# Attention inside a hybrid trunk step: heads taken in order 0, 2, 1, 3, scores issued as pairs of two key heads, values as stationary operand, and the result left transposed for the output projection

## The reference

```python
HEAD_DIM = 64; ATTN_HEADS = 4; KV_HEADS = 2; ATTN_BLOCK = 128; WINDOW = 128
...
def one_block(b):
    parts = [einsum('bqkgd,bckd->bkgqc', qblk, k_ctx)]                # 128 context keys
    if local:                                                        # latent queries only
        s_loc = einsum('bqkgd,bskd->bkgqs', qblk, k_blk)             # up to 3 x 128 keys
        parts.append(where(valid, s_loc, -inf))
    p = softmax(concatenate(parts + [sink_logit], axis=-1), axis=-1)
    out = einsum('bkgqc,bckd->bqkgd', p[..., :c_len], v_ctx)
    if local:
        out = out + einsum('bkgqs,bskd->bqkgd', p[..., c_len:...], v_blk)
    return out
```

## Time and profile before

| | |
|---|---|
| median of 3 runs | 1483.44 us (1482.91 to 1487.77) |
| span of the profiled execution, first to last instruction | 1481.4 us |
| PE busy | 1254.5 us, 85% of the span |
| DVE, ACT, POOL busy | 709.7, 282.3, 114.1 us |
| chain that ended last | PE 53%, DMA 24%, DVE 11% |
| granted TensorE clock, mean | 0.927 |

### The profile page before, as it was taken

How to read it: one execution, slowest core, us unless ns; L and a number is a source line. 1 busy time by engine, 2 the same in 40 slices (tenths; PEclk the granted TensorE clock), 3 DMA queues, 4 the chain that set the end, 5 groups by cost and what they waited for, 6 DMA issues and landing times.

```text
span 1481.4 us, 20556 instructions
## 1 busy us (share of the span) xinstructions
PE 1254.5 (85%) x7762; PEld 864.0 (58%) x7762; DVE 709.7 (48%) x1579; ACT 282.3 (19%) x708; POOL 114.1 (8%) x171
## 2 busy tenths in 40 slices
PE   5999999888986797998849999988799579889792
PEld 2765577657862565565437556766578356465550
DVE  2256866782356132332363686677443633223324
ACT  0211132651111000000022104256211100000000
POOL 2000000001000211111000000000100011111100
PEclk9999999999987898999979999999999679899996
DMA  9221101247049999999761110014822389999985
GB/s 383 117 89 44 70 1 57 112 185 295 29 168 361 386 415 420 420 418 418 311 242 47 71 57 29 1 67 170 344 84 97 132 349 413 420 419 416 412 333 233
DMA packets 58179, 334.61 MB, mean 226 GB/s; under 512 B 11392, under 2 KB 11392, under 8 KB 23900
## 3 DMA queue, kind: packets, MB, share of 16 engines
q1 hardware_dynamic: 42336, 294.94, 49.4%
q0 software_dynamic: 15744, 38.34, 6.7%
HBM read 322.41 MB, written 27.61 MB: 236 GB/s over the span
## 4 chain that ended last, share of the span: by engine, by line
PE 53%; DMA 24%; DVE 11%; issue 4%; ACT 3%; DVEq 2%; SPq 1%; PEld 1%; ACTq 0%; POOL 0%; PEldq 0%; POOLq 0%
DMA U<-in_stream 14%; PE bank L1664 12%; PE bank L2033 10%; PE bank L1600 8%; PE bank L1923 7%; PE bank L2067 5%; DMA ring<-in_stream 5%; DMA RAB<-mod_rows 2%; PE bank L1765 1%; PE bank L1939 1%; DVE U L1203 1%; PE bank L1705 1%; DMA U<-moe_out 1%; PE bank L2015 1%; SPq L350 1%
## 5 line engine op out<-in xcount | busy, mean ns | idle before, releaser
L2033 PE MATMUL bank<-U,HT 128*64 128x256 f32 (+2 forms) x1248 | 211.6, 415 | 27.5 <-DMA U<-in_stream 22.8
L2033 PEld LDWEIGHTS bank<-U,HT 128*64 128x64 f32 (+2 forms) x1248 | 142.0, 154 | 82.7 <-issue 54.4
L1664 PE MATMUL bank<-HT,ring 128*128 128x512 f32 (+1 forms) x640 | 175.4, 435 | 2.1 <-issue 2.1
L1923 PE MATMUL bank<-ring,HT 128*128 128x256 f32 x640 | 150.6, 397 | 14.6 <-DVE U L1254 9.0
L1600 PE MATMUL bank<-ring,HT 128*128 128x256 f32 x640 | 151.7, 390 | 6.0 <-ACT HT L603 4.2
L1923 PEld LDWEIGHTS bank<-ring,HT 128*128 128x128 f32 x640 | 127.0, 201 | 34.8 <-issue 11.2
L1664 PEld LDWEIGHTS bank<-HT,ring 128*128 128x128 f32 x640 | 97.3, 191 | 79.8 <-issue 79.8
L1600 PEld LDWEIGHTS bank<-ring,HT 128*128 128x128 f32 x640 | 121.2, 195 | 23.0 <-ACT HT L603 4.1
L2033 PE MATMUL bank<-ring,HT 128*64 128x256 f32 (+2 forms) x608 | 119.8, 418 | 14.3 <-DMA ring<-in_stream 11.7
L1043 DVE SCALAR_TENSOR_TENSOR U<-U,prm 128x655 f32<-128x655 f32 x120 | 107.8, 898 | 5.9
L2067 PE MATMUL bank<-ring,HT 128*64 128x512 f32 (+2 forms) x224 | 100.3, 625 | 5.1 <-DMA U<-in_stream 5.1
(11 more groups left out here) (347 smaller groups left out, 1614.0 us busy)
## 6 DMA issues: line engine op xcount, KB each, us to landing
ring<-in_stream SPq DMA_DIRECT2D x140, 1024.0 KB, 10.3
U<-in_stream SPq DMA_DIRECT2D x108, 1024.0 KB, 17.1
RAB<-in_stream SPq DMA_DIRECT2D x18, 1024.0 KB
U<-moe_out SPq DMA_DIRECT2D x20, 512.0 KB, 7.3
RAB<-mod_rows POOLq DMA_DIRECT2D x12, 512.0 KB, 11.9
moe_in<-CAT POOLq DMA_DIRECT2D x10, 512.0 KB, 2.9
X<-in_x SPq DMA_DIRECT2D x1, 2560.0 KB, 15.3
out_y<-X SPq DMA_DIRECT2D x5, 512.0 KB, 6.8
```

The source lines that it names most:

```text
L1664: ins = e.matmul(out, wt(q)[:, k, P * (n % 2):P * (n % 2) + P], HT[:, k, lo:lo + w], start=(k == 0), stop=(k == KD - 1))
L1923: ins = e.matmul(PS[4 + n % 2][:, 256 * j:256 * j + 256], HT[:, k, t * P:(t + 1) * P], wt(q + j)[:, k, :], start=(k == 0), stop=(k == KD - 1))
L2033: ins = e.matmul(PS[2 + p][s, FF * j:FF * j + FF], xgT[:, p, k, s], wt(key)[:, k, :], start=(k == 0), stop=(k == KD - 1))
```

## The change

`HEADS = (0, 2, 1, 3)` is the order in which heads are taken. `scores(t, g)` issues the products of query heads g and 2 + g together, which use key heads 0 and 1 and so partitions 0 to 63 and 64 to 127, into two banks. `values(t)` is one call for a block: the value columns of a key head are the stationary operand (64 columns) and the transposed probabilities of its two query heads move (256 columns), so that the result stands transposed in bank 5, one key head on each half of the partitions. Since a per-query factor then runs along the free axis, `factors(t)` spreads the inverted sums over 64 partitions by four products with the identity, ACT copies them to `facs`, and DVE multiplies by them. The first two pieces of the concatenated result are already transposed, so the output projection reads them from CAT; the rows of its weight are permuted to fit on the host. Waits on one bank or another move with this (`att_fs` in place of `pj_sb` for the gate's banks), and some semaphores are joined.

```diff
-        PTs = view(TMP + 2048, 2, 4, P)
+        PTs = (view(TMP + 2048, 4, 2, P), view(2560 + 4 * 512, 4, 2, P))
+        facs = view(TMP + 3072, 2 * P)
...
+        def factor_bank(t):
+            return PS[6 + t % 2] if t + 1 < NT else PS[3]
...
                 for t in range(NT):
-                    for h in range(QH):
-                        if t:
-                            e.wait_ge(S["att_pt"], 20 * l + 4 * (t - 1) + h + 1)
-                        A(Pm[:, h, 0:w], PS[h][:, 0:w], ACT.Exp, ...)
-                    A(es[:, t, :], es[:, t, :], ACT.Exp).then_inc(S["att_es"], 1)
+                    for h in HEADS[:3]:
+                        exps(t, h)
+                    probs_out(t, HEADS[0])
+                    exps(t, HEADS[3])
+                    A(es[:, t, :], es[:, t, :], ACT.Exp).then_inc(S["att_exp"], 1)
                     e.wait_ge(S["pj_ps"], 10 * l + NT + t + 1)
                     A(CAT[:, t, 256:768], PS[6 + t % 2][:], ACT.Copy).then_inc(S["pj_sb"], 1)
-                    probs_out(t, 0)
                     if t == NT - 1:
-                        for n in range(3):
+                        for n in range(2):
                             columns_out(n)
-                    probs_out(t, 2)
+                    probs_out(t, HEADS[2])
+                    if t == NT - 1:
+                        columns_out(2)
+                    e.wait_ge(S["att_f"], NT * l + t + 1)
+                    A(facs, factor_bank(t)[:, 0:256], ACT.Copy).then_inc(S["att_fs"], 1)
...
+                    tap(2)
+                    probs_out(t, HEADS[1])
+                    e.wait_ge(S["att_exp"], 25 * l + 5 * t + 5)
+                    e.tensor_tensor(den, sums[:, t, :], es[:, t, :], ALU.add); dr()
+                    e.reciprocal(rden, den).then_inc(S["att_den"], 1)
...
+                    e.wait_ge(S["att_pv"], NT * l + t + 1)
+                    e.wait_ge(S["att_fs"], NT * l + t + 1)
+                    e.tensor_tensor(CAT[:, t, 0:256], PS[5][:, 0:256], facs, ALU.mult).then_inc(S["att_o"], 1)
...
+                def factors(t):
+                    if t:
+                        e.wait_ge(S["att_o"], NT * l + t)
+                    e.wait_ge(S["att_den"], NT * l + t + 1)
+                    e.wait_ge(S["pj_sb"], 10 * l + NT + t + 1)
+                    for g in range(2):
+                        for kv in range(KVH):
+                            ins = e.matmul(factor_bank(t)[64 * kv:64 * kv + 64, g * P:(g + 1) * P],
+                                           rden[:, 2 * kv + g:2 * kv + g + 1].to_broadcast((P, HD)), ident[:], ...)
...
+                def values(t):
+                    nb = [0] if t == 0 else [-1] + near(t)
...
                     for i, j in enumerate(nb):
-                        ins = e.matmul(PS[5][:, 64 * h:64 * h + 64], PTs[:, h % 2, i, :], v, ...)
+                        for kv in range(KVH):
+                            k = slice(64 * kv, 64 * kv + 64)
+                            ins = e.matmul(PS[5][k, 0:256], v, PTs[kv][:, i].rearrange("p a b -> p (a b)"), ...)
...
-                    turned_tile(t, "ct_ps", ("ct_sb_a", "ct_sb_d"), (0, 1, 6, 7, 2, 3, 4, 5))
+                    turned_tile(t, "ct_ps", ("ct_sb_a", "ct_sb_d"), (6, 7, None, None, 2, 3, 4, 5))
...
+                            rows = CAT[:, t, k * P:(k + 1) * P] if k < 2 else HT[:, k, t * P:(t + 1) * P]
```

More of the change, by code:

```diff
@@ L38 @@
 ROUNDS = list("PPFPFQBPBPPFBQBBPP")
+HEADS = (0, 2, 1, 3)
 SLOT = 2048
@@ L1091, in tap @@
                     done[0] = min(62, done[0] + n)
-                for h in range(QH):
+                for h in HEADS:
                     att_max(0, h)
@@ L1693, in _, with scores @@
                 e.wait_ge(S["ch_sb"], 8 * (l + 1))
[L1695 to L1698 removed]
+                def scores(t, g):
+                    rows = [(kv, slice(64 * kv, 64 * kv + 64), PS[2 * kv + g]) for kv in range(KVH)]
                     if t == 0:
[L1700 removed]
+                        for kv, r, bank in rows:
+                            ins = e.matmul(bank[:, 0:P], qkT[r, g, 0:P], qkT[r, 2, 0:P], start=True, stop=True)
                     else:
@@ L1766, in head @@
                     ins.then_inc(S["att_pv"], 1)
-                for h in range(QH):
-                    scores(0, h)
+                rden = small(108, QH)
+                for g in range(2):
+                    scores(0, g)
                 for i in range(4):
@@ L1772, in _ @@
                 for t in range(NT):
-                    for h in range(QH):
-                        head(t, h)
+                    if t + 1 < NT:
+                        fill = [lambda i=i: gate_part(4 * t + 4 + i) for i in range(4)]
+                    else:
+                        fill = [lambda i=i: columns(i) for i in range(4)]
+                    turned_probs(t, HEADS[0])
+                    fill[0]()
+                    turned_probs(t, HEADS[1])
+                    if t + 1 < NT:
+                        scores(t + 1, 0)
+                    else:
+                        fill[1]()
+                    turned_probs(t, HEADS[2])
+                    if t + 1 < NT:
+                        fill[1]()
+                    else:
+                        fill[2]()
+                    turned_probs(t, HEADS[3])
+                    if t + 1 < NT:
+                        scores(t + 1, 1)
+                    factors(t)
+                    fill[2 if t + 1 < NT else 3]()
+                    values(t)
+                    if t + 1 < NT:
+                        fill[3]()
+                columns(4)
                 columns(5)
```

140 lines of the change are left out of this document (63 added, 77 removed).

## The result

The changed kernel takes 1464.34 us (median of 4 runs, 1459.94 to 1466.35) against 1483.18 us for the kernel before (4 runs, 1482.83 to 1487.77) on the same chip. The quotient of these two medians is 0.9873. The ratio on record is 0.9842, with a 95% interval of 0.9817 to 0.9867; the record doesn't say how its runs are weighted. So the saving is 18.8 us by the medians and 23.4 us by the ratio. The forecast was 1461.1 in a range of 1453 to 1471, a ratio of 0.985.

What follows compares the result with a forecast made beforehand. TensorE's instructions were taken to bound attention blocks 0 to 3. Savings of 9.0 + 1.7 (last block) + 0.45 (projection) = 11.15 us a layer, 22.3 in all, gave 1461.1 us, range 1453 to 1471.

Steps and rivals of the forecast that it cites:

- case (a): Whole run: half-array products overlap and the whole saving reaches the end; 1461.1 us, range 1453 to 1467, chance 0.73.
- Blocks 0 to 3: Attention's first four query blocks, bound by TensorE: savings of 1.19, 2.45, 2.90 and 2.46 us, together 9.0 a layer.
- 0.15 for the turn, so 0.51: Context part of a score pair: 0.36 us for four alternating records plus 0.15 for turning to half rows, against 0.82.
- The rule on packs: Context pair by the skill's rule, one matmul plus some 4 ns a tile: 0.22 us, whole sum near 1456.5.
- Rival (c): Attention scores: pairs do not overlap, columns do; 2.5 + 4.3 us a layer lost, 1474.7 us, chance 0.07.
- Factors: Each attention block: four added products of 64 by 128, eight records, cost 0.50 us; alone they would be 0.88.
- Last block, to L1830: Last attention block, decided by hand-offs: 9.6 us against 10.46 before, with TensorE waiting 1.9 for ScalarE's gate copy.
- TensorE's own 2.2 us end last, and 0.7 goes: Barrier before the mixer: VectorE, last by 0.72 us, finishes earlier, so TensorE ends last and 0.7 us is saved.
- Projection: Output projection: two of eight transposes go per block; only the last two blocks' count, 4 x 0.11 = 0.45 us.
- Rival (b): Attention blocks 1 to 3: VectorE's copy or the exponential becomes the wait, beyond 1.5 us margin; 1470 us, chance 0.12.
- Rival (d): Attention: neither row nor column halves overlap; 3.85 us a layer more, 1491 us, chance 0.04.
- Rival (e): Last attention block: granted clock falls to 1.2 GHz; some 3 us a layer lost, 1468 us, chance 0.04.

Runs made afterwards that it cites:

- e2: Changed kernel with each score pair issued one key head after the other (context, latent, masks), same products and banks; 1482.79 us, ratio 0.9979.
- e9: Changed kernel with the output projection transposing eight pieces per block again, two of them unread; 1464.31 us, ratio 0.9843.
- e7: Changed kernel with score products and value products both issued one key head after the other; 1487.29 us, ratio 1.0.
- a2: The changed kernel run again, nothing edited, beside the kernel before on its own chip; 1461.35 us, ratio 0.9841.
- a3: The changed kernel run once more, unedited, in another set beside the kernel before; 1462.54 us, ratio 0.9842.
- e1: Changed kernel with ScalarE's gate copy moved ahead of its first probability copy in every block; 1457.02 us, ratio 0.9815.
- g2: Repeat, in another set, of the changed kernel with ScalarE's gate copy ahead of its first probability copy; 1462.78 us, ratio 0.9829.
- g3: Changed kernel with the gate copy first and the second of ScalarE's three last copies done by VectorE; 1459.59 us, ratio 0.9809.
- e3: Changed kernel with the value products of key head 0 over all key blocks first, then those of key head 1; 1470.22 us, ratio 0.9884.
- e4: Changed kernel with each block's four factor products issued twice; 1472.43 us, ratio 0.9889.

## Why the prediction was right, step by step

The time and the likeliest case (a) were right: TensorE's price in blocks 0 to 3, brought down by overlap, and passed on to the end. The sum came out nearly right too, in part by luck, since its terms were off in both directions.

- **Blocks 0 to 3, 9.0 a layer forecast, 9.85 measured** (1.53 + 2.73 + 3.10 + 2.49). Shown, since undoing the overlap gives the gain back. The step "0.15 for the turn, so 0.51" for the context pair was mis-sized: it made the narrow pair dearer than one head (0.41 in the same view), and the pair costs no more than one head. Context and latent pair together take 1.07 us where 0.51 + 0.65 = 1.16 was forecast. By their starts the eight pairs save 7.6 us where 6.8 was forecast. The value groups save 0.4 more than forecast and the factors cost 0.36 more; transposes, gate and masks come out even. The rule on packs that was weighed there (the Trainium skill, "TensorE: Matmul & The Clock Gate", Part 3) has a pack cost about what one of its tiles costs, which e2 bears out for this pair (0.33 for one head and 0.32 to 0.33 for two), but not its total of 1456.5, since it had 0.22 as the price of one. Latent pairs (one head's price) and values (1.88 forecast, 1.88 measured) were right. Rival (c), pairs that don't overlap, was not the case; e2, which takes their overlap away, prices it at 8.45 us a layer where 6.8 was forecast.
- **Factors, 0.50 forecast, 0.58 measured**, and 0.44 for a repeated set: the shape's pace was right, the start on top of it was missed.
- **Last block, to L1830: 9.6 forecast, 9.76 measured** at full clock, with the wait of 1.9 forecast at 1.77. The step that fell is "TensorE's own 2.2 us end last, and 0.7 goes": 3.22 became 2.94 or 2.95, so 0.27. ScalarE's copies of the product end last at the barrier and moving one of them away gains only 0.05. Together 0.97 a layer, not 1.7.
- **Projection, 0.45 forecast, 0.43 measured** (e9). The other six transposes were worth nothing, as said: the gate vector ends that stage. That the stage would last 1.2 and 1.6 us less in the profile after was in no term, and why it did is open.
- **Rival (b)**, VectorE, was not the case: one more tap per block costs 0.28 us a layer, two cost 2.4. The margin of 1.5 us was right for block 2 (1.4), and too wide for blocks 1 (0.7) and 3 (1.2).
- **Rival (d)**, no overlap at all and slower, 1491 forecast. With both orders undone the kernel ties with the one before (ratio 1.0). e7 is not quite that rival: the rival had no overlap of columns at all, while column halves that stand one behind the other still overlap partly, and the factors were left in turns (0.58 a block, not 0.88).
- **Rival (e)**, the lower clock in the last block, was put at 3 us a layer with a chance of 0.04. It happened in layer 0 of three of four profiled executions with this attention, and cost 0.83 us (the profile after), 1.16 (a2) and 1.14 (e9); layer 1 and both layers of a3 were free of it. So it was far likelier than forecast and far cheaper, and that it did no harm to the sum is luck. The condition for being wrong, "if the last block grows past 10.5 us", was met in all three (10.59, 10.92, 10.90), but by the clock and not by the hand-offs. That the wait of 1.77 us brings the fall on is argued, not shown: of the 20 last blocks with it 11 had a fall, of the six without it (e1, g2, g3) none.
- **The sum of 22.3 against the runs.** At full clock the attention and the projection give 2 x (9.85 + 0.97 + 0.43) = 22.5 us, the sum forecast within 0.2. What the runs gained is less certain than that: 18.8, 25.6 and 29.1 us between the medians of the three sets, where the kernel before alone ranges from 1477.25 to 1495.74, and 23.4 by the ratio. The spans of the profile after and of before differ by 16.8. There 20.8 came from the attention, 2.8 from the wait stages and 0.4 net from the start and the end; the mixers at a lower clock took 5.1 back and the rest of layer 0 2.1. Only the attention and the projection's 0.9 were in the sum. a3, whose attention was free of a lower clock, gives 22.0, but there too 2.7 from the wait stages happened to cover the 2.4 of the mixers. That the median of the first set is short of the sum by such falls of the clock is argued from profiled executions, not shown.
- **The stream of tiles moved**, as it had to: the longest wait of layer 0's experts, 29.46 us from 702.15, is 29.63 us from 694.33 after. By then the execution was 7.8 us ahead, of the 11 us a layer that was forecast; the mixer of that layer had taken 3.6 back.

## What to carry to other kernels

Products that fill half of the array (64 rows of keys, or 64 columns of values) should be issued in turns, a product of the other half behind each: two then cost about one, and here the order of two loops is the whole difference between a ratio of 0.984 and one of 1.0. When adding up a change on the busiest engine, price the start of a group apart from its pace, and look at which engine's last copy ends a barrier before counting what the others give up. And when runs differ by several microseconds, compare the stage's starts in the trace: most of these repeat within 0.02 us at full clock and told 0.2 us apart where the medians could not tell 1.5.

## What the hardware showed that was not expected

- **Column halves run ahead of one another.** In e3 the second half's products began while the first half's were still in the list (2.79 us for the group, against 1.88 in turns and 16 x 0.215 = 3.44 with no overlap), and the same in e7. Whether rows would do the same no run shows: in e2 the masks, which use the whole array, stand between the two heads' products.
- **The clock of the same mixer differs within one execution.** 59.19 us in one layer of e4 and 64.80 in the other, behind waits that are equal. The Trainium skill ("TensorE: Matmul & The Clock Gate", Part 1) says that the same kernel can show different counts of slow matmuls at its start from one run to the next. These traces show such a difference far from the start, and between the two layers of one run, of up to 5.6 us a mixer. Nothing here says which of two layers will be hit.
- **The gate vector's way through memory** took 6.52 + 12.72 us before and 5.86 + 12.18 after in layer 0 (write out, read back; the way back spreads each row over all partitions, 512 KB a transfer). The wait stage built on it lasted 25.5 us in both layers before. Of the 26 such stages in the profiled executions behind the change 20 took 23.9 to 24.4 us, two 24.8 and 24.9, and four 25.2 to 25.5. With one profiled execution of the kernel before, whether its place in time has a part in this stays open.
